# Two transformer blocks on one core: weight splits further ahead on ScalarE, the attention maps combined without normalising the first, head squares on ScalarE

## What is computed

```python
h = rmsnorm(x, pre_mix_w); proj = h @ w_in            # 1024 x 5120
# differential attention, 4 heads, two maps each, value width 128
s = q @ k.T * scale - slope * dist
p = softmax(s)
a = p[:, :, 0] - lam * p[:, :, 1]
o = rmsnorm(a @ v, subln_w) * (1.0 - lambda_init)     # over the 128 columns of a head
# neighbourhood attention, 8 heads of width 64, with a bias table
merged = g_a * (y_a @ w_branch_a) + g_b * (y_b @ w_branch_b)
x = x + rmsnorm(merged @ w_out, post_mix_w)           # then the feed-forward part, then the second block
```

## Time and profile before

| | us |
|---|---|
| median of three runs | 812.2 |
| lowest, highest run | 810.98, 813.88 |
| the profiled execution, its own time | 810.16 |
| its span, from the first to the last instruction | 808.4 |
| TensorE busy in the span | 779.1 (96%) |
| VectorE busy | 480.5 (59%) |
| ScalarE busy | 400.1 (49%) |
| GpSimd busy | 58.0 (7%) |

### The profile page before, as it was taken

How to read it: one execution, slowest core, us unless ns; L and a number is a source line. 1 busy time by engine, 2 the same in 40 slices (tenths; PEclk the granted TensorE clock), 3 DMA queues, 4 the chain that set the end, 5 groups by cost and what they waited for, 6 DMA issues and landing times.

```text
span 808.4 us, 10499 instructions
## 1 busy us (share of the span) xinstructions
PE 779.1 (96%) x4019; PEld 646.1 (80%) x4019; DVE 480.5 (59%) x731; ACT 400.1 (49%) x584; POOL 58.0 (7%) x128
## 2 busy tenths in 40 slices
PE   8999899999999999999999979999999999999996
PEld 7887677878788788988878857777888888889885
DVE  5575665568666656654364566645677466566533
ACT  6445455463545454634354635556545445444531
POOL 2200000000280000000040010100002000000000
PEclk9999999999999999999999989999999999999999
DMA  8765343364566556554645524433365566555641
GB/s 301 245 208 183 104 157 105 105 207 147 200 209 187 161 174 203 194 166 165 218 113 155 191 95 125 151 117 108 102 200 156 181 193 207 175 173 176 208 131 52
DMA packets 55072, 134.34 MB, mean 166 GB/s; under 512 B 6839, under 2 KB 12142, under 8 KB 55022
## 3 DMA queue, kind: packets, MB, share of 16 engines
q1 hardware_dynamic: 54512, 132.34, 51.2%
q10 hardware_dynamic: 510, 1.33, 0.5%
HBM read 132.60 MB, written 1.05 MB: 165 GB/s over the span
## 4 chain that ended last, share of the span: by engine, by line
PE 80%; DVE 8%; ACT 6%; issue 4%; POOL 1%; DMA 1%; SPq 0%; ACTq 0%; DVEq 0%; POOLq 0%
PE acc L973 72%; PE aux L921 4%; ACT weights_high L617 3%; DVE weights_low L1219 3%; ACT probs L772 1%; DVE probs L1455 1%; PE aux L1071 1%; PE aux L1038 1%; DMA weights_raw<-in_w_in_dram 1%; PE aux L1143 1%; PE aux L1050 1%; DVE gates L1289 0%; PE aux L1173 0%; PE aux L1178 0%; DVE probs L1471 0%
## 5 line engine op out<-in xcount | busy, mean ns | idle before, releaser
L1219 DVE SCALAR_TENSOR_TENSOR weights_low<-weights_raw,gain_columns,weights_high 128x1024 fp32r<-128x1024 f32 (+4 forms) x189 | 219.4, 1194 | 73.8 <-ACT weights_high L617 73.6
L973 PE MATMUL acc<-weights_high,h_high 128*128 128x512 f32 (+4 forms) x768 | 235.3, 387 | 6.4 <-ACT weights_high L617 3.1
L973 PE MATMUL acc<-weights_low,h_high 128*128 128x512 f32 (+4 forms) x768 | 227.1, 377 | 2.7 <-DVE weights_low L1219 2.3
L973 PE MATMUL acc<-weights_high,h_low 128*128 128x512 f32 (+4 forms) x768 | 226.6, 376 | 0.0
L617 ACT ACTIVATE weights_high<-weights_raw,gain_columns 128x1024 fp32r<-128x1024 f32 (+4 forms) x189 | 194.9, 1073 | 7.4 <-DMA weights_raw<-in_w_in_dram 5.5
L973 PEld LDWEIGHTS acc<-weights_low,h_high 128*128 128x128 f32 x768 | 139.6, 188 | 32.2 <-DVE weights_low L1219 6.2
L973 PEld LDWEIGHTS acc<-weights_high,h_low 128*128 128x128 f32 x768 | 140.2, 188 | 27.1 <-DVE h_low L1238 0.4
L973 PEld LDWEIGHTS acc<-weights_high,h_high 128*128 128x128 f32 x768 | 136.5, 189 | 31.3 <-ACT weights_high L617 4.1
L1216 DVE TENSOR_TENSOR weights_low<-weights_raw,weights_high 128x1024 fp32r<-128x1024 f32 x68 | 80.8, 1221 | 38.3 <-ACT weights_high L617 38.1
L617 ACT ACTIVATE weights_high<-weights_raw 128x1024 fp32r<-128x1024 f32 x68 | 69.1, 1056 | 45.1 <-DMA weights_raw<-in_ffn_w_down_dram 20.9
L1678 POOL TENSOR_SCALAR stats<-stats 128x1 f32<-128x1 f32 (+1 forms) x17 | 8.0, 468 | 681.9 <-ACT row L630 304.1
(11 more groups left out here) (240 smaller groups left out, 688.5 us busy)
## 6 DMA issues: line engine op xcount, KB each, us to landing
weights_raw<-in_w_in_dram SPq DMA_DIRECT2D x64, 512.0 KB, 4.9
weights_raw<-in_w_down_dram SPq DMA_DIRECT2D x22, 512.0 KB, 4.6
weights_raw<-in_ffn_w_down_dram SPq DMA_DIRECT2D x22, 512.0 KB, 4.4
weights_raw<-in_w_gate_dram SPq DMA_DIRECT2D x40, 256.0 KB, 3.4
weights_raw<-in_w_up_dram SPq DMA_DIRECT2D x40, 256.0 KB, 4.1
weights_raw<-in_ffn_w_gate_dram SPq DMA_DIRECT2D x40, 256.0 KB, 3.4
weights_raw<-in_ffn_w_up_dram SPq DMA_DIRECT2D x40, 256.0 KB, 4.2
weights_raw<-in_w_out_dram SPq DMA_DIRECT2D x16, 512.0 KB, 4.0
```

Of the source, the lines that this page charges most:

```text
L973: i = nc.tensor.matmul(acc[:, 2 * t + b, 0:width], lhs[:, k0, sl], w[:, u % RING, base + d:base + d + width], start=(kt == 0 and n == 0), ...
L1219: i = nc.vector.scalar_tensor_tensor(lo[:, u % RING, c], raw[:, u % RING, c], gcol[:, g:g + 1], hi[:, u % RING, c].bitcast(F32), ALU.mult, ...
```

## The change

Four edits, all within the first block's attention.

1. ScalarE splits units with a lead of 2.2 products in the four matrices named in `EARLY`, where it was 0.8. VectorE's lead stays 0.
2. `combine` no longer divides the first map by its sum s1. It makes r = -lambda * s1 / s2 and then e1 + r * e2 in one pass, from the unnormalised exponentials. The map is then s1 times the former one, and the norm behind it takes the factor out: `da_norm` uses 1e-6 * s1 * s1. It grows from two GpSimd instructions to five, on 4 columns.
3. The squares of `da_out` are taken by ScalarE, from PSUM, right behind the copy; VectorE's `da_squares` goes, and the bank is free when the squares are read.
4. `turn_y` of `da` comes one slot later (slots 10 and 14, before 9 and 13).

```diff
+EARLY = {"v_a_q_b": 2.2, "k_b_v_b": 2.2, "gate_a": 2.2, "gate_b": 2.2}
...
-        q[i + 4].append(do("da_squares", i))
         if i % 4 == 3:
             q[i + 4].append(do("da_norm", i // 4))
             q[i + 5].append(do("da_heads", i // 4))
-            q[i + 6].append(do("turn_y", "da", i // 4))
+            q[i + 7].append(do("turn_y", "da", i // 4))
...
@@ ScalarE, step "da_out"
+                    if i >= 2:
+                        act.wait_ge(*at("sumsq", ("da_head", i - 2)))
+                    junk = lam_in[:, 2 * (i % 2):2 * (i % 2) + 2, :].rearrange("p a b -> p (a b)")
+                    nc.scalar.activation(junk, aux[bank_of["da", i]][:, 0:P], ACT.Square,
+                                         accum_out=stat(("ss", ("da", qt)), 4)[:, n:n + 1])\
+                        .then_inc(*tick("sumsq", ("da_head", i)))
...
@@ ScalarE, main loop
-                    advance(ahead_of(i, 0.8))
+                    advance(ahead_of(i, EARLY.get(st[1], 0.8)))
...
@@ TensorE, step "pv"
-                    reader[bank] = ("act", ("da_out", i)) if kind == "da" else ("vec", ("heads", kind, i))
+                    reader[bank] = ("sumsq", ("da_head", i)) if kind == "da" else ("vec", ("heads", kind, i))
...
@@ VectorE, step "distance": lambda with its sign turned
-                    then(nc.vector.tensor_tensor(lam[:, 2:3], lam[:, 0:1], lam[:, 1:2], ALU.subtract))
+                    then(nc.vector.tensor_tensor(lam[:, 2:3], lam[:, 1:2], lam[:, 0:1], ALU.subtract))
...
@@ VectorE, step "combine"
-                    r = stat(("rsum", i), 2)
+                    r = stat(("ratio", i))
                     c = 2 * (i % 4)
-                    then(nc.vector.reciprocal(r, stat(("sum", "da", i // 4), 8)[:, c:c + 2]))
-                    then(nc.vector.tensor_scalar(r[:, 1:2], r[:, 1:2], lam[:, 2:3], None, ALU.mult))
-                    then(nc.vector.tensor_scalar(T[:, 256:512], T[:, 256:512], r[:, 1:2], None, ALU.mult))
-                    signal(nc.vector.scalar_tensor_tensor(T[:, 0:256], T[:, 0:256], r[:, 0:1], T[:, 256:512],
-                                                          ALU.mult, ALU.subtract), "vec", ("combined", i))
-                elif kind == "da_squares":
...
-                    signal(nc.vector.tensor_tensor_reduce(
-                        out=junk, in0=o, in1=o, scale=1.0, scalar=0.0, op0=ALU.mult, op1=ALU.add,
-                        accum_out=stat(("ss", ("da", qt)), 4)[:, n:n + 1]), "sumsq_vec", ("da_head", i))
...
+                    both = stat(("sum", "da", i // 4), 8)
+                    then(nc.vector.reciprocal(r, both[:, c + 1:c + 2]))
+                    then(nc.vector.scalar_tensor_tensor(r, both[:, c:c + 1], lam[:, 2:3], r, ALU.mult, ALU.mult))
+                    signal(nc.vector.scalar_tensor_tensor(T[:, 0:256], T[:, 256:512], r, T[:, 0:256],
+                                                          ALU.mult, ALU.add), "vec", ("combined", i))
...
@@ GpSimd, step "da_norm"
-                    rstd("sumsq_vec", ("da", a[0]), GLA_DV, 4)
+                    key = ("da", a[0])
+                    pool.wait_ge(*at("sumsq", key))
+                    first = stat(("sum", "da", a[0]), 8).rearrange("p (n c) -> p c n", c=2)[:, 0, :]
+                    e, ms = stat(("eps", key), 4), stat(("ms", key), 4)
+                    then(g.tensor_tensor(e, first, first, ALU.mult))
+                    then(g.tensor_scalar(e, e, EPS, 0.0, ALU.mult, ALU.add))
+                    then(g.tensor_scalar(ms, stat(("ss", key), 4), 1.0 / GLA_DV, 0.0, ALU.mult, ALU.add))
+                    then(g.tensor_tensor(ms, ms, e, ALU.add))
+                    done(g.tensor_tensor(stat(("rstd", key), 4), ms, half[:, 0:4], ALU.pow), "rstd", key)
```

More of the change, by code:

```diff
@@ L236, in timeline @@
             q[15 + i].append(do("turn_y", "na", i // 4))
-    FIRST_OF = ("q_b_turn", "k_b_turn", "pv", "da_out", "heads_out", "turn_p", "combine", "score", "da_squares",
+    FIRST_OF = ("q_b_turn", "k_b_turn", "pv", "da_out", "heads_out", "turn_p", "combine", "score",
                 "da_norm", "da_heads", "turn_y")
@@ L794, in step @@
                                          ACT.Copy).then_inc(*tick("act", ("da_out", i)))
+                    if i >= 2:
[4 more added lines that the diff above has]
+                        .then_inc(*tick("sumsq", ("da_head", i)))
+                    if n == 3:
+                        marks["sumsq", ("da", qt)] = counts["sumsq"]
                 elif kind == "turn_y":
@@ L1406, in step @@
                     dve.wait_ge(*at("act", "lambda_exp"))
-                    then(nc.vector.tensor_tensor(lam[:, 2:3], lam[:, 0:1], lam[:, 1:2], ALU.subtract))
-                    signal(nc.vector.tensor_scalar(lam[:, 2:3], lam[:, 2:3], 0.8 - 0.6, None, ALU.add), "vec", "lambda",
-                           True)
+                    then(nc.vector.tensor_tensor(lam[:, 2:3], lam[:, 1:2], lam[:, 0:1], ALU.subtract))
+                    signal(nc.vector.tensor_scalar(lam[:, 2:3], lam[:, 2:3], -(0.8 - 0.6), None, ALU.add), "vec",
+                           "lambda", True)
                 elif kind == "norm_turn":
@@ L1466, in step @@
                         dve.wait_ge(*at("vec", "lambda"))
-                    r = stat(("rsum", i), 2)
+                    r = stat(("ratio", i))
                     c = 2 * (i % 4)
-                    then(nc.vector.reciprocal(r, stat(("sum", "da", i // 4), 8)[:, c:c + 2]))
-                    then(nc.vector.tensor_scalar(r[:, 1:2], r[:, 1:2], lam[:, 2:3], None, ALU.mult))
-                    then(nc.vector.tensor_scalar(T[:, 256:512], T[:, 256:512], r[:, 1:2], None, ALU.mult))
-                    signal(nc.vector.scalar_tensor_tensor(T[:, 0:256], T[:, 0:256], r[:, 0:1], T[:, 256:512],
-                                                          ALU.mult, ALU.subtract), "vec", ("combined", i))
-                elif kind == "da_squares":
[L1476 to L1482, removed]
-                    signal(nc.vector.tensor_tensor_reduce(
-                        out=junk, in0=o, in1=o, scale=1.0, scalar=0.0, op0=ALU.mult, op1=ALU.add,
-                        accum_out=stat(("ss", ("da", qt)), 4)[:, n:n + 1]), "sumsq_vec", ("da_head", i))
-                    if n == 3:
-                        marks["sumsq_vec", ("da", qt)] = counts["sumsq_vec"]
+                    both = stat(("sum", "da", i // 4), 8)
[3 more added lines that the diff above has]
+                                                          ALU.mult, ALU.add), "vec", ("combined", i))
                 elif kind == "da_heads":
```

## The result

| | before | after |
|---|---|---|
| median, us | 812.53 | 799.5 |
| lowest, highest run | 810.98, 813.88 | 798.64, 800.19 |
| the profiled execution, its own time | 810.16 | 800.11 |
| its span | 808.4 | 798.4 |
| its mean granted clock | 0.994 | 0.989 |

The changed kernel takes 0.984 of the time, with a 95% interval of 0.9818 to 0.9862: 13 us less in the medians, 10 us in the two profiled executions. Forecast were 801.7 us, within a range of 798.5 to 807.0.

The account below looks back on a forecast made before the run. TensorE, 96% busy, was held by waits between ScalarE and VectorE; slots 4 to 14 falling from 59.1 to 48.5 us gain 10.5, giving 799.7 us profiled, plus 2.0 for the median: 801.7 us, range 798.5 to 807.

Parts of the forecast that it names:

- The ring, cut by the lead: First block's attention: exponentials, high part, low part, combine, next scores take 5.41 us a turn; the lead cuts this wait cycle.
- Rival 2: First block's attention: low parts still await their own slot's high part, only combine is shorter; 809 us, chance 0.04.
- TensorE's slots: Slots 4 to 14 at TensorE's own pace: 48.5 us instead of 59.1, a gain of 10.5 us.
- a whole `da` slot 4.41: TensorE's own work in one attention slot (pv, turn_p, score, two products), taken as 4.41 us without a stop.
- Own work of the other engines: Per attention slot: VectorE 2.8 us, ScalarE 3.2 us, both less than TensorE's 4.41, so TensorE sets the pace.
- `turn_y`, `combine`, squares at nothing: First block's attention: once VectorE has slack, shorter combine and moved squares gain nothing; later turn_y avoids slot 13's 1.8 us wait.
- rival 3: ScalarE changes its function table around each square in eight slots; gain gone, 812 us, chance 0.01.
- the 1.8 us kept for the range: Slot 14: turn_y might wait for VectorE's late copy as in slot 13; priced 0, with 1.8 us in the range.
- `da_norm`: GpSimd, two to five instructions: at most 7.4 us in a 7.5 us window, so it costs nothing.
- Raw weights: Loads for ScalarE's earlier splits: issued 11 us or more ahead, slowest landing 9.2 us, so no cost.
- Rival 4: ScalarE stands for late raw weights, stopping all three engines; slower, 815 us, chance 0.02.
- one of my two signs of being wrong: From slot 15 on: prediction wrong if that stretch becomes longer; the other sign was TensorE idle over 3 us, slots 4 to 14.

Follow-up runs that it names:

- all_but_lead: Changed kernel with ScalarE's lead of 2.2 put back to 0.8, the other edits kept: 809.4 us, ratio 0.9967 to the kernel before.
- act_load2: Changed kernel plus two unused 512-column copies on ScalarE in each da_out: 799.18 us, ratio 0.9843 to the kernel before.
- act_load4: Changed kernel plus four unused 512-column copies on ScalarE in each da_out: 807.52 us, ratio 0.9949 to the kernel before.
- lead_only: Kernel before with only ScalarE's lead of 2.2 added: 799.67 us, ratio 0.986 to the kernel before.
- turn_early: Changed kernel with turn_y of da back in slots 9 and 13: 800.09 us, ratio 0.9857 to the kernel before.
- low_ahead: Changed kernel, lead also in second block, there ScalarE 4.2 in gla_og, latent, gate_a2 and VectorE 2.0: 799.26 us, ratio 0.9848 to before.
- high_4_2_early: Changed kernel, lead also in second block, there ScalarE 4.2 in gla_og, latent, gate_a2, VectorE's lead unchanged: 799.63 us, ratio 0.9851 to before.
- lead_turn: Kernel before with ScalarE's lead of 2.2 and turn_y one slot later, nothing else: 800.92 us, ratio 0.9864 to the kernel before.
- lead_4_2: Changed kernel with ScalarE's first-block lead at 4.2 instead of 2.2: 799.53 us, ratio 0.9845 to the kernel before.

## Why the prediction was right

**The ring, cut by the lead.** Right, and shown: the lead alone gives the whole gain, all but the lead leaves the ring at 5.02 us. Rival 2 had priced a ring that stays closed at 809 us; `all_but_lead` took 809.4.

**TensorE's slots.** The sum was 48.5 us for slots 4 to 14; they took 122.67 - 74.81 = 47.9. The term that was mis-sized is "a whole `da` slot 4.41": it measured 4.28. I had taken one slot of the kernel before as a whole; the pieces of the chain after (0.44, 0.22, 0.86, 2.75) add up to 4.27. The slot that I took was not without a stop. In it `turn_p` could load its weights only when the combined map was done (start us, us, in the kernel before):

```profile
70.34 0.49 DVE L1472 SCALAR_TENSOR_TENSOR probs<-probs,stats 128x256 f32<-128x256 f32 x1
70.88 0.20 PEld L1050 LDWEIGHTS aux<-ident,probs 128*128 128x128 f32 x2
```

That is 0.74 us behind the first weights of `pv` (70.14), where after it is 0.57 (74.41 to 74.98). Slots 4 to 7 took 17.11 us where I had 17.64, and slots 8 and 9 3.44 and 3.85 for 3.55 and 3.99. Slots 10 to 14 were within 0.05 us each. The 59.1 us of the kernel before were slightly wrong too: they run from a start on the timeline to one in the chain, and by one view alone it is 58.9. Slot 15 begins 11.2 us earlier where 10.5 were forecast, and 0.7 us before the 123.4 I gave.

**Own work of the other engines.** VectorE's 2.8 us a slot measured 2.9 (4.28 less the 1.40 idle). ScalarE's 3.2 us a slot was a little high (2.8), and the free 1.2 us a little low (1.5); `act_load2` and `act_load4` put the bound between 1.2 and 2.5 us. The square at 0.35 us measured 0.25.

**`turn_y`, `combine`, squares at nothing.** Right, by `lead_only` and `turn_early`. Nor did the squares change ScalarE's table (rival 3): both traces have five table loads, none of them between 5 and 240 us. In slot 14 `turn_y` (119.44) stands in the chain without a wait, so the 1.8 us kept for the range were not needed.

**`da_norm`.** Nothing, as forecast, and with far more room: 2.1 us against the bound of 7.4. The rule of the Trainium skill (GPSIMD Engine Reference, section 8, Key points) on contention for SBUF beside two-input work of VectorE barely came to bear in the kernel after. The first four instructions end before VectorE's next low part begins at 85.63 us; the power starts within 0.02 us of it and takes 1.02 us, as it does (1.01) where no low part runs. That was a matter of place. In `act_load2` the first instruction came 0.08 us behind the start of a low part, and took 1.26 us instead of 0.20, while the low part kept its 1.28:

```profile
86.28 1.28 DVE L1233 SCALAR_TENSOR_TENSOR weights_low<-weights_raw,gain_columns,weights_high 128x1024 fp32r<-128x1024 f32 x1
86.36 1.26 POOL L1768 TENSOR_TENSOR stats<-stats 128x4 f32<-128x4 f32 x1 [60.56 <-ACT lambda_in L804]
```

There the trace agrees with the rule, for GpSimd and not for VectorE. All five then took 3.2 us, still inside the 7.5 us of the window, and nobody waited for them.

**Raw weights.** Right for this change: no such wait between 70 and 120 us, not even at 4.2. Rival 4's mechanism exists all the same, one place further on, as `low_ahead` and `high_4_2_early` show: with 11.5 to 12.2 us of waits, 5 us are lost.

**Behind slot 15.** From the start of slot 15 to the turn of `merged` it took 53.3 us instead of 53.9, the end of `gate_b` that I had left standing. From there to the end it took 622.4 us instead of 620.6. So the stretch from slot 15 on became longer, 675.7 us where it was 674.6, and that was one of my two signs of being wrong. The traces place the loss. Where the clock falls in both kernels, from 448.49 to 487.92 us before and from 436.78 to 476.23 after, the same matmuls take 39.4 us in both. But from 548.43 to 570.85 us before they take 22.4 us, and from 536.82 to 560.79 after 24.0. TensorE stops briefly in that stretch in both executions; only in the one after did the clock fall behind the stop. Windows before:

```profile
558.00:560.00 2.00, 0.48 (x3) 0.33 (x3) 1.33 (x2) 2.00 (x3) 0.00 (x0) 1.00 0.65 246
560.00:562.00 2.00, 2.00 (x15) 1.78 (x14) 1.26 (x8) 1.77 (x6) 0.00 (x0) 1.00 0.00 0
```

After:

```profile
546.00:548.00 2.00, 0.48 (x3) 0.08 (x2) 0.95 (x1) 2.00 (x3) 0.00 (x0) 1.00 0.81 231
548.00:550.00 2.00, 2.00 (x5) 1.63 (x6) 1.38 (x7) 1.76 (x5) 0.00 (x0) 0.57 0.07 27
550.00:552.00 2.00, 2.00 (x11) 1.83 (x10) 0.46 (x2) 1.58 (x4) 0.00 (x0) 0.58 0.00 0
```

It goes with the execution, not with the change. `turn_early`, `lead_turn`, `lead_4_2` and the two `act_load` kernels have the same second block, no fall of the clock there, 22.4 us for those matmuls, and 674.0 to 674.1 us from slot 15 on. `lead_only` has the fall, and takes 24.0 and 675.5 us. So behind slot 15 nothing got worse, and 0.5 us were gained. Why the clock falls in one execution and not in another stays open.

**The number.** 11.2 and 0.6 us gained, 1.8 lost, of which 1.6 are that fall of the clock: 10.0 us of span, so the profiled execution took 800.1 where I had 799.7. That these lie within 0.4 us of each other is partly luck, since a gain priced 0.7 us too low and 0.6 us left out met a loss that no term of mine had. The median was forecast 2.0 us above the profiled execution and lies 0.6 below. So the miss of 2.2 us in the median is that offset of the kernel before, 2.6 us off, less the 0.4; I carried it over to another kernel, where nothing fixes it.

## What to carry to other kernels

Where two engines in strict order each make half of something and a third consumes it, look for the ring: a period in the chain of waits that is longer than any engine's own work in it. Here, moving one half a single step ahead gave all there was, while trimming the operations in the ring gave their own length per turn and nothing once it was cut. Such a lead must be bounded by when the loads land, place by place: the same 4.2 products cost nothing in one stretch and 5 us in another. And before a microsecond is put down to a change, look whether other executions with the same code have it: here 1.6 us did not belong to the change.

## What the hardware showed unexpectedly

- Reading the sum of an activation is nearly free: an activation of 128 columns with its sum took 0.25 us to the next start, the plain copy before it 0.17.
- A GpSimd instruction that started just behind a low part on VectorE was held until about its end: 1.26 us instead of 0.20 in `act_load2`. So the power of 1.47 us in the earlier trace rows, of one column, was no price of the power. It ran while VectorE did low parts; where none was running the same power took 0.56 us. For 4 columns it took 1.02 us.
- A short stop of TensorE can cost clock behind it, but need not. In the kernel after, TensorE was busy 1.3 of the 4 us from 456 to 460, and then ran at half its clock until close to 470. Behind the stop near 547 us (0.48 of 2 us busy) the clock fell in two executions, of `after` and `lead_only`, and not in seven others with the same second block. In the kernel before, 8.5 us of idle time spread over 59 to 126 us left it at 1.00.
- Time at half clock need not cost anything. With 10 us of it around 465 us the same matmuls took 39.4 us, as with 7; some 3 us of it near 549 us went with a loss of 1.6.
